# Seven modulation vectors of a two-layer diffusion backbone: from 32-column matmuls beside the attention to weighted sums on VectorE beside the Fourier transform and the gated projection

## The reference, cut to what matters

```python
def ada_params(cond, w, b):                    # cond: 1024 numbers, w: 1024 x 6144
    m = jax.nn.silu(cond) @ w + b
    return jnp.split(m, N_MOD, axis=-1)        # sh_m, sc_m, g_m, sh_f, sc_f, g_f

for i in range(DEPTH):                         # DEPTH = 2
    sh_m, sc_m, g_m, sh_f, sc_f, g_f = ada_params(c, ada_w[i], ada_b[i])
    h_l = modulate(rmsnorm(x, norm_mix_w[i]), sh_m, sc_m)
    ...
    y_l = ab_mixer(...) if i % 2 == 0 else sgu_mixer(...)   # attention + Fourier | gated MLP
    x = x + g_m * y_l
    x = x + g_f * peer_ffn(modulate(rmsnorm(x, norm_ffn_w[i]), sh_f, sc_f), ...)
```

## Time and profile before

| | us |
|---|---|
| median of 3 runs | 2876.34 |
| the runs | 2873.65 to 2881.97 |
| the profiled execution | 2879.16 |
| its span, first to last instruction | 2877.4 |
| attention phase (119.0 to 254.5 of the span) | 135.5 |
| Fourier phase (254.5 to the first matmul of `about`, 294.3) | 39.8 |
| gsin (1499.0 to the first matmul of `sgu`, 1613.6) | 114.6 |
| the two expert FFNs and the rest | some 2590 |

### The profile page before, as it was taken

How to read it: one execution, slowest core, us unless ns; L and a number is a source line. 1 busy time by engine, 2 the same in 40 slices (tenths; PEclk the granted TensorE clock), 3 DMA queues, 4 the chain that set the end, 5 groups by cost and what they waited for, 6 DMA issues and landing times. The chain is left out here.

```text
span 2877.4 us, 36364 instructions
## 1 busy us (share of the span) xinstructions
PE 2625.8 (91%) x12550; PEld 2152.7 (75%) x12550; DVE 1984.0 (69%) x4269; ACT 1029.4 (36%) x2922; POOL 1363.0 (47%) x1092
## 2 busy tenths in 40 slices
PE   6999799999999999999948789999999999999992
PEld 3644578888888878888836658788888887878881
DVE  4463379988777756666673447998877775666667
ACT  4352232288788400000014332239878830000000
POOL 1000053656667746655531025365677674555562
PEclk9999899999999999999979899999999999999996
DMA  8282325999999999999972134599999999999995
GB/s 327 96 347 109 118 89 214 389 360 355 388 409 409 407 404 409 409 409 409 409 282 73 66 111 147 209 402 357 357 396 409 409 407 405 409 409 409 409 409 206
DMA packets 246304, 916.84 MB, mean 319 GB/s; under 512 B 27089, under 2 KB 32241, under 8 KB 238833
## 3 DMA queue, kind: packets, MB, share of 16 engines
q0 software_dynamic: 147456, 536.94, 47.5%
q1 hardware_dynamic: 94512, 373.49, 33.4%
q10 hardware_dynamic: 4160, 4.19, 0.4%
HBM read 908.22 MB, written 6.29 MB: 318 GB/s over the span
## 5 line engine op out<-in xcount | busy, mean ns | idle before, releaser
L1463 PE MATMUL exp_down<-peer_gates,all_ring 128*128 128x256 f32 x2720 | 613.6, 382 | 25.6 <-DMA all_ring<-in_peer_v 25.4
L1436 PE MATMUL exp_out<-peer_both,all_ring 128*128 128x256 f32 x2752 | 620.8, 381 | 13.6 <-DMA all_ring<-in_uT 12.5
L1463 PEld LDWEIGHTS exp_down<-peer_gates,all_ring 128*128 128x128 f32 x2720 | 508.1, 190 | 122.1 <-DMA all_ring<-in_peer_v 55.7
L1436 PEld LDWEIGHTS exp_out<-peer_both,all_ring 128*128 128x128 f32 x2752 | 516.1, 191 | 89.8 <-DMA all_ring<-in_uT 21.6
L1354 POOL DMA_INDIRECT all_xT<-in_u_rows,peer_eidx x278 | 365.5, 1315 | 158.2 <-DVE peer_dots L1812 94.3
L1819 DVE SCALAR_TENSOR_TENSOR peer_both<-all_xT,peer_dots,peer_both 128x1024 f32<-128x1024 f32 x226 | 290.4, 1285 | 143.5 <-DMA all_xT<-in_peer_v,peer_eidx 133.9
L1812 DVE CUSTOM_DVE_ANT_0 all_xT<-all_xT,peer_both 128x1024 f32<-128x1024 f32 x278 | 337.6, 1222 | 62.0 <-DMA all_xT<-in_u_rows,peer_eidx 51.8
L1354 POOL DMA_INDIRECT all_xT<-in_peer_v,peer_eidx x230 | 261.2, 1136 | 183.9 <-DVE peer_both L1819 149.8
L1463 PE MATMUL exp_down<-peer_gates,spare_ring 128*128 128x256 f32 x1376 | 314.7, 382 | 10.6 <-DMA spare_ring<-in_peer_v 10.5
L1563 ACT ACTIVATE spare_heavy<-all_iota_b,spare_index 128x128 f32<-128x128 bf16 x1024 | 314.2, 410 | 0.0
L1436 PE MATMUL exp_out<-peer_both,spare_ring 128*128 128x256 f32 x1344 | 305.0, 380 | 2.4 <-DMA spare_ring<-in_uT 2.4
(11 more groups left out here) (298 smaller groups left out, 3829.4 us busy)
## 6 DMA issues: line engine op xcount, KB each, us to landing
all_ring<-in_uT SPq DMA_DIRECT2D x172, 512.0 KB
all_ring<-in_peer_v SPq DMA_DIRECT2D x170, 512.0 KB
mix_raw<-in_ada_tiles SPq DMA_DIRECT2D x48, 1024.0 KB, 9.6
spare_ring<-in_peer_v SPq DMA_DIRECT2D x86, 512.0 KB
spare_ring<-in_uT SPq DMA_DIRECT2D x84, 512.0 KB
all_ring<-in_w_peer_q SPq DMA_DIRECT2D x22, 512.0 KB, 3.4
all_ring<-in_w_gs_in SPq DMA_DIRECT2D x16, 512.0 KB, 3.2
all_ring<-in_w_in SPq DMA_DIRECT2D x10, 512.0 KB
```

Of the source, the lines that this page charges most:

```text
L1436: mm = nc.tensor.matmul(outs[:, c % 2, 0:DENSE], raw[c % R][:, k, :], hd[:, k, :], start=(k == 0), stop=(k == KD - 1))
L1463: mm = nc.tensor.matmul(dn[:, m, :], raw[at % R][:, m, :], gates[:, :, c, :], start=(c == 0 and m % 2 == 0), stop=(c == NKEYS - 1), skip_g ...
```

## The change

Vectors 2 to 4 stay in the attention phase (9 steps, `COUNT = 5`). Vectors 5 to 7 are summed in the Fourier phase (`SUMMED = 8`), vectors 8 to 11 in gsin. A summed vector takes on DVE 8 passes over 128 x 1024 (`weigh_row`: one multiply, then seven multiply-adds, each waiting for the one before), with the weight per partition from `column`, a new 128 x 8 tile that ACT makes in `front`; on PE 8 matmuls with the sums as 128 x 128 weights and two moving columns of ones (`fold_columns`), which do both the sum over partitions and the turn; on DVE the bias. `bias` and `column` lie in a room that lasts the whole program. In gsin the 16 MB come in 16 chunks of 1 MB into three buffers, and the loops over tiles are written out.

```diff
+def weigh_row(nc, to, row, scalar, k):
+    if k == 0:
+        return nc.vector.tensor_scalar(to, row, scalar, None, ALU.mult)
+    return nc.vector.scalar_tensor_tensor(out=to, in0=row, scalar=scalar, in1=to, op0=ALU.mult, op1=ALU.add)
+
+def fold_columns(nc, bank, sums, ones):
+    for m in range(KD):
+        mm = nc.tensor.matmul(bank[:, 2 * m:2 * m + 2], sums[:, m * P:(m + 1) * P], ones[:, 0:2], start=True, stop=True)
+    return mm
 class Modulations:
     FIRST = 2
-    COUNT = DEPTH * N_MOD
+    COUNT = 5
+    SUMMED = 8
...
+    def fold(self, pe, v):
+        pe.wait_ge(self.s_sum, KD * (v - self.COUNT + 1))
+        pe.wait_ge(self.s_taken, v)
+        fold_columns(self.nc, self.bank, self.sums[v % 2], self.ones).then_inc(self.s_mm, self.STEPS)
# attention_phase, SP
+            for v in range(mods.COUNT, mods.COUNT + 2):
+                sp.wait_ge(mods.s_mm, mods.STEPS * (v - 2) + 2)
+                mods.load(sp, v)
# fourier_phase, SP, PE, DVE
+            for v in range(mods.COUNT + 2, mods.SUMMED):
+                sp.wait_ge(mods.s_sum, KD * (v - 1 - mods.COUNT))
+                mods.load(sp, v)
...
                 mm.then_inc(s_y, 1)
+                if 1 <= g < FG - 1:
+                    mods.fold(pe, mods.COUNT + g - 1)
+            mods.fold(pe, mods.SUMMED - 1)
...
                 if g >= 1:
                     low(g - 1)
+                if g >= 2:
+                    mods.take_vector(dve, mods.COUNT + g - 2)
+                for step in range(6 * g, 6 * g + 6):
...
+                    mods.sum_step(dve, step)
             low(FG - 1)
+            mods.take_vector(dve, mods.SUMMED - 1)
# entry_phase (gsin), SP, PE, DVE
+            for c in range(3):
+                load_part(c)
+            for m in range(2, tiles):
+                sp.wait_ge(s_lo, m - 1)
+                sp.dma_start(ring[m % 2][:, :, :], w[m]).then_inc(s_in[m % 2], 16)
+                if m + 1 < CHUNKS:
+                    load_part(m + 1)
...
+                mm.then_inc(s_mm, 1)
+                if m in FOLD_AT:            # after tiles 5, 9, 13
+                    fold(FOLD_AT[m])
+            fold(VECTORS - 1)
...
+            for c in range(2):
+                sum_part(c)
+            for m in range(2, tiles):
+                split_lo(m // 2, m % 2)
+                sum_part(m)
+                if m - 1 in FOLD_AT:
+                    take_vector(FOLD_AT[m - 1])
+            take_vector(VECTORS - 1)
```

More of the change, by code:

```diff
@@ L337, in _ @@
             act.activation(mods.cond[:, :, 1], small[:, ROW_CCTX:ROW_CCTX + KD], ACT.Silu).then_inc(s_cond, 1)
+            act.activation(mods.column[:, :], small[:, ROW_C:ROW_C + KD], ACT.Silu).then_inc(s_cond, 1)
             def flatten(v):
@@ L610, in _, with entry_phase @@
                     mm.then_inc(s_mm, 1)
-def entry_phase(nc, tag, ring, w, tiles, src, weight, shift, scale, hi, lo, ones, eps, take_act):
+def entry_phase(nc, tag, ring, w, tiles, src, weight, shift, scale, hi, lo, ones, eps, vectors, take_act):
     with Room(nc, tag) as r:
@@ L625, in entry_phase @@
         total = r.ps("total", [P, 512])
+        ada_tiles, first_v, ada, bias, column = vectors
+        VECTORS = DEPTH * N_MOD - first_v
+        CHUNKS = VECTORS * KD // 2
+        part = [r.sb(f"part{j}", [P, 2, D]) for j in range(3)]
+        sums = [r.sb(f"sums{j}", [P, D]) for j in range(2)]
+        bank = r.ps("bank", [P, 512])
+        s_part = [r.sem(f"part_in{j}") for j in range(3)]
+        s_vsum, s_fold, s_vector = (r.sem(x) for x in ("vector_sum", "folded", "vector_taken"))
         s_in = [r.sem(f"in{j}") for j in range(2)]
@@ L629, in entry_phase @@
         s_hi, s_lo, s_mm, s_out = (r.sem(x) for x in ("hi", "lo", "multiplied", "taken"))
+        FOLD_AT = {4 * i + 5: i for i in range(VECTORS - 1)}
         block = r.block()
@@ L635, in _, with load_part @@
                 sp.dma_start(ring[j][:, :, :], w[j]).then_inc(s_in[j], 16)
-            with sp.Fori(1, tiles // 2) as it:
-                for j in range(2):
-                    sp.wait_ge(s_lo, it * 2 + j - 1)
-                    sp.dma_start(ring[j][:, :, :], w[bass.ds(it * 2 + j, 1)].rearrange("o p k n -> (o p) k n")
-                                 ).then_inc(s_in[j], 16)
+            def load_part(c):
+                if c >= 3:
+                    sp.wait_ge(s_vsum, 2 * (c - 2))
+                k = c % (KD // 2) * 2
+                sp.dma_start(part[c % 3][:, :, :], ada_tiles[first_v + c // (KD // 2)][:, k:k + 2, :]
+                             ).then_inc(s_part[c % 3], 16)
+            for c in range(3):
[5 more added lines that the diff above has]
+                    load_part(m + 1)
         @block.gpsimd
@@ L729, in _, with sum_part, take_vector @@
             split_lo(0, 1)
-            with dve.Fori(0, tiles // 2 - 1) as it:
-                for j in range(2):
-                    split_lo(it + 1, j)
+            def sum_part(c):
+                dve.wait_ge(s_part[c % 3], 16 * (c // 3 + 1))
+                i = c // (KD // 2)
+                for h in range(2):
+                    k = c % (KD // 2) * 2 + h
+                    if k == 0 and i >= 2:
+                        dve.wait_ge(s_fold, i - 1)
+                    elif k > 0:
+                        dve.wait_ge(s_vsum, 2 * c + h)
+                    weigh_row(nc, sums[i % 2][:, :], part[c % 3][:, h, :], column[:, k:k + 1], k).then_inc(s_vsum, 1)
+            def take_vector(i):
+                dve.wait_ge(s_fold, i + 1)
+                at = slice((first_v + i) * KD, (first_v + i + 1) * KD)
+                nc.vector.tensor_tensor(ada[:, 0, at], bank[:, 0:2 * KD].rearrange("p (m c) -> p c m", c=2)[:, 0, :],
+                                        bias[:, at], ALU.add).then_inc(s_vector, 1)
+            for c in range(2):
+                sum_part(c)
+            for m in range(2, tiles):
+                split_lo(m // 2, m % 2)
[3 more added lines that the diff above has]
+            take_vector(VECTORS - 1)
+            dve.wait_ge(s_vector, VECTORS)
 def residual(nc, xT, gate):
@@ L1893, in program @@
         ada = r.sb("ada", [P, 2, DEPTH * ADA_ROWS])
+        bias = r.sb("bias", [P, DEPTH * ADA_ROWS])
+        column = r.sb("column", [P, KD])
         ident = r.sb("ident", [P, P])
```

47 lines of the change are left out of this document (32 added, 15 removed).

## The result

| | before | changed |
|---|---|---|
| median, us | 2878.38 (6 runs, 2871.22 to 2882.45) | 2901.53 (6 runs, 2899.15 to 2905.67) |
| ratio, 95% interval | 1 | 1.0079 (1.0065 to 1.0092) |
| profiled execution | 2879.16 | 2899.19 |
| granted clock over the span | 0.966 | 0.959 |

What follows compares the result with a forecast made beforehand. PE was taken to bound the attention's second part and the Fourier phase, also after vectors move. Attention -8.7, Fourier +6.4 and gsin +9.0 sum to +6.7 us; from the median of 2876.3 that gives 2883.0, range 2872 to 2892.

Steps and rivals of the forecast that it cites:

- The expert FFNs are not touched: Expert FFNs: the change does not reach them, so they add nothing to the sum.
- The test that I had set: Whole kernel: if the three changed phases' sum differs from the whole by over 3 us, the expert FFNs were reached.
- Gain 8.7: Attention: 17.0 us gained at full clock, less 8.3 us for a slower PE clock.
- The sum of the price: Attention: PE's clock falling to 1.2 GHz costs between 0 and 17.0 us, taken as 8.3.
- the values: Attention, three blocks of values: about 3.4 us of each runs slow and costs 1.7, 5.1 us in all.
- the pairs: Attention, pairs of units: 0.4 us more per pair of 640 keys, 0.65 of 512; about 3.2 us taken.
- Rival 1: Attention: PE's clock holds at 2.4 GHz, gain 17.0, total -3.6 us, 2873; chance 0.15.
- rival 4: Attention: waits at the values go too, at most -7.8 on top of Rival 1, 2865; chance 0.04.
- rival 2: Attention: clock stays at 1.2 GHz from unit 11 on, gain about 0, total +15 to +17, 2892; chance 0.18.
- The turns and the end: gsin: three turns between tiles on PE, 5.7 us, and a fourth ending the phase, +1.3.
- contention: gsin's start: VectorE's first passes lengthen POOL's last two low halves by 1 us each, +2.0, between 0 and 2.6.
- Rival 3: gsin: VectorE becomes the bound and splits come late; 1 us lost on 14 tiles gives 2897; chance 0.05.

Runs made afterwards that it cites:

- e1_shift: Kernel before, with bias and an unused column in the whole-program room, every later tile 416 B higher, no instruction added: 2892.52 us, ratio 1.0052.
- e2_place: Changed kernel with bias and column behind the ring tiles, so all tiles keep their place modulo 128 B: 2888.10 us, ratio 1.0047.
- e11_after_spread: Changed kernel with POOL's first eight row fetches issued two at a time after splits 11 to 14 of each asking part: 2890.68 us, ratio 1.0029.
- e6: Changed kernel with every tile set on a multiple of 64 B: 2898.08 us, ratio 1.0067.
- e10_late_sums: e2_place, with VectorE in gsin waiting for POOL's last low half before its first four passes: 2886.04 us, ratio 1.0020.
- e12: e2_place plus weight tiles at 128 modulo 256 B, row fetches two at a time, and gsin's first sums behind POOL's low halves: 2881.10 us, ratio 1.0006.
- e5: Kernel before, with every tile set on a multiple of 64 B: 2880.14 us, ratio 1.0011.
- e7: Kernel before, with weight tiles of about, gsin, gsout and the asking parts at 128 modulo 256 B: 2887.58 us, ratio 1.0037.
- e8_rel0_spread: e7, with POOL's first eight row fetches two at a time after splits 11 to 14 of the asking parts: 2873.66 us, ratio 0.9997.

## Why the prediction was wrong

**The sign was right, the size was not**: 2883.0 with 2872 to 2892 was forecast, 2901.5 came. The step that failed is the sentence "The expert FFNs are not touched", a term of nothing that stood for +15.1 in the profile. I had compared instructions, and there the FFNs are the same; I had not compared addresses, though the text says itself that `bias` and `column` move to a room that lasts the whole program. `e1_shift` shows that the addresses alone cost the kernel before 15.9 us, `e2_place` that the asking parts are as before once the tiles are back in place, `e11_after_spread` that about 14 us of the 23 go with the holds behind queued splits. The test that I had set, a difference of over 3 us between the three phases and the whole, is met with 17.7 (20.0 - 2.3). Without the placement (`e2_place`) the change costs 11.5 us by the medians, still more than 6.7. The profiled executions, 8.8 us apart, show 1.4 too much in gsin and some 1 us each in the front, gsout and the start of FFN 1; these last three no run explains.

**Attention.** Gain 8.7 forecast, 13.7 in the profiled execution, but 10.0, 6.9, 7.3, 6.7 and 7.4 in the five other kernels with the same attention (`e2`, `e6`, `e10`, `e11`, `e12`): 8.7 on average of the six. The profiled one began with a first ten units 2.5 us quicker than before, where no instruction differs. All six are set against one execution of before, and the four other kernels with the old attention lie at +2.8, +2.8, -2.4 and -1.0 (`e1`, `e5`, `e7`, `e8`), so the gain is known to 1 or 2 us at best.

The sum of the price held: from the eleventh to the last normalisation 82.1 us before, 65.2 by the sum at full clock, 67.9 in the changed kernel and 70.9 to 71.5 in the others, so 2.7 to 6.3 us; and from the last normalisation to the Fourier phase 7.7 before and 10.8 to 11.2 after, +3.1 to +3.5. Price 5.8 to 9.8, against 8.3. Its terms did not hold, and that they made up for each other is luck. For the values I took 3 x 1.7, from 3.4 us at half clock in each block, which no row of before shows; the changed kernel has 4.51, 4.51 and 5.57 us, that is 0, 0 and +1.9, and the other five 0 to +0.7, 0 and +1.9 to +2.3. For the pairs I took 3.2, at 0.4 us for one of 640 keys, from the row at 164.81 in the earlier trace rows, which I read as one at 1.2 GHz; the granted clock in 164.8 to 166.8 is 0.66. In `e2_place`, where 198 to 214 is wholly at half clock, the same scores take 1.65 us instead of 1.08:

```profile
199.74 1.65 PE L883 MATMUL attn_ps_s<-mix_mixT 64*128 64x384 f32 x4
```

A late unit of 640 keys there comes 3.94 us after the one before, 1.1 more than 2.85 and not 0.4. Against that, the first step of the sum (from the eleventh to the twelfth normalisation) and the last took 1.4 us less than summed. Nor is the end after the last normalisation all the change's: in `e1`, `e5`, `e7` and `e8`, with the old attention, it is 9.3 to 10.7 us, with the last values at a clock of 0.59 to 0.70; the profiled execution of before, with 1.00, is the exception.

Rival 1, with the clock up, did not come (0.80), nor rival 4; rival 2's clock came in part (0.63 to 0.74 in other kernels), without its price. The rule of the Trainium skill on transposes ("TensorE: Matmul & The Clock Gate", Part 4: PE-mode transpose) would have put all of the stretch but the values at 1.2 GHz; the means of 0.63 to 0.80 lean that way, and the gain was not 0.

**Fourier phase.** 6.4 forecast and 6.4 measured (6.3 to 7.9 in the others that have it), with PE waiting 1.15 us for the last pass. From the first copy to the end of the last pass it took 37.3 us instead of 38.0, and the last turn, behind that wait, 2.5 instead of 1.9: the exact hit is partly chance.

**gsin.** 9.0 forecast, 9.8 to 10.8 measured from its first matmul. The turns and the end are 7.2 (`e10_late_sums`) against 7.0. The term that was too small is contention: 1.9 to 3.2 instead of 2.0, since I took only the wait (1.3) and not the clock behind it. Rival 3, a late split, did not come: no wait of PE for `w_lo`. My estimate of +2.6 by the rule of the Trainium skill on the shared pair ("SBUF — State Buffer", Who interferes with whom) counted only the waits, too.

**Front.** Nothing forecast, +2.3 measured. Its weight tiles moved off their good place, 0.683 to 0.700 for three matmuls, which on some 80 triples is 1.4 us; the rest is within what one execution is uncertain by.

The rule of the Trainium skill on the shared pair bears on the FFNs more than on gsin. The rows show a small pass of two inputs, or a CAST or TENSOR_SCALAR, ending with POOL's split at 441.6, 1811.5 and in the three places of `e1_shift`. MAX8 and FIND_INDEX8 beside a split are not held, as in `e8_rel0_spread`, where the third row, a TENSOR_TENSOR of usually 0.19 us, is held for what is left of the same split:

```profile
1783.82 0.27 DVE L1646 MAX8 top_val<-ask_kept 128x8 f32<-128x128 f32 x1
...
1784.07 0.28 DVE L1649 FIND_INDEX8 ask_idx<-top_val,ask_kept 128x8 uint32<-128x128 f32 x1
...
1785.19 1.01 DVE L1687 TENSOR_TENSOR top_cand<-top_val 128x32 f32<-128x32 f32 x1
```

```profile
1783.77 2.39 POOL L1331 TENSOR_TENSOR ask_w_lo<-all_ring,ask_w_hi 128x1024 fp32r<-128x1024 f32 x1 [0.33 <-ACT ask_w_hi L1495]
```

The Trainium skill ("SBUF — State Buffer", Who interferes with whom) says that the pair is held for a whole instruction against a pass with two inputs in SBUF; that cast and tensor_scalar, with one, can contend as well, in the modes that use both ports; and that other passes with at most one input do not. The trace agrees: 0.27 and 0.28 us against 1.01, and 2.45 and 2.39 for the CAST and the TENSOR_SCALAR of `e1_shift`.
